# Two norms in a row computed from one pair of sums, and gate weights that stand still in TensorE, on one core

## The reference, cut to what matters

```python
# end of the first block
h = h + g2 * swiglu(hn, ffn_w1[1], ffn_w3[1], ffn_w2[1])
x = rms_norm(h, final_g)                 # x: the residual that the second block adds to
# start of the second block
xn = rmsnorm(x, norm_mix_2)              # rmsnorm(x, g) = x * rsqrt(mean(x*x) + 1e-6) * g
# xn @ w_in_2 gives, among others:
#   keys and values for compression      (feature tiles 12 to 15 of what is called f1 here)
#   the queries and the other keys       (feature tiles 0 to 11 of f1)
#   64 gate columns: beta, decay, head gates (called tm0 here)
```

## Time and profile before

| | |
|---|---|
| median of 3 runs | 1251.72 us (1245.33 to 1254.25) |
| the profiled execution | 1253.79 us, span 1252.0 us |
| PE busy | 1175.9 us, 94% |
| DVE busy | 815.5 us, 65% |
| ACT busy | 590.6 us, 47% |
| POOL busy | 77.7 us, 6% |
| DMA | 226.41 MB, mean 181 GB/s |
| mean granted TensorE clock | 0.964 of full |

### The profile page before, as it was taken

How to read it: one execution, slowest core, us unless ns; L and a number is a source line. 1 busy time by engine, 2 the same in 40 slices (tenths; PEclk the granted TensorE clock), 3 DMA queues, 4 the chain that set the end, 5 groups by cost and what they waited for, 6 DMA issues and landing times.

```text
span 1252.0 us, 24371 instructions
## 1 busy us (share of the span) xinstructions
PE 1175.9 (94%) x10460; PEld 1119.1 (89%) x10460; DVE 815.5 (65%) x1487; ACT 590.6 (47%) x1085; POOL 77.7 (6%) x94
## 2 busy tenths in 40 slices
PE   5888799999996999999997999998999999999999
PEld 2687689999995999999997888887998999899999
DVE  3874759988885566554454578887764575777543
ACT  2434546445445444444444466763333355556442
POOL 0000010000011000000100001111520001000000
PEclk9889999999998999999698899998999999999999
DMA  9660638898891647642244242221212555755520
GB/s 389 266 256 2 258 146 346 342 357 319 333 349 43 232 170 274 202 172 69 72 182 171 75 142 70 102 102 68 70 37 85 185 183 188 272 199 202 185 107 13
DMA packets 32363, 226.41 MB, mean 181 GB/s; under 512 B 3584, under 2 KB 4736, under 8 KB 5120
## 3 DMA queue, kind: packets, MB, share of 16 engines
q1 hardware_dynamic: 30528, 221.20, 47.6%
q10 hardware_dynamic: 1728, 3.67, 0.8%
HBM read 223.80 MB, written 1.05 MB: 180 GB/s over the span
## 4 chain that ended last, share of the span: by engine, by line
PE 82%; DVE 9%; ACT 5%; DMA 2%; issue 1%; POOL 0%; SPq 0%; DVEq 0%; ACTq 0%; POOLq 0%
PE bank L546 21%; PE bank L548 20%; PE bank L547 20%; DVE sb_wlo L1772 3%; ACT sb_whi L1302 2%; PE bank L989 2%; PE bank L651 1%; PE bank L584 1%; DVE sb_ring L1806 1%; DMA sb_ring<-in_f 1%; PE bank L574 1%; DMA sb_ring<-in_ada 1%; PE bank L564 1%; PE bank L1011 1%; PE bank L980 1%
## 5 line engine op out<-in xcount | busy, mean ns | idle before, releaser
L546 PE MATMUL bank<-sb_xh,sb_whi 128*128 128x256 f32 x1496 | 427.7, 286 | 8.1 <-DVE sb_wlo L1772 5.6
L547 PE MATMUL bank<-sb_xl,sb_whi 128*128 128x256 f32 x1496 | 420.8, 281 | 0.0
L548 PE MATMUL bank<-sb_xh,sb_wlo 128*128 128x256 f32 x1496 | 420.6, 281 | 0.0
L1772 DVE TENSOR_TENSOR sb_wlo<-sb_ring,sb_whi 128x1024 fp32r<-128x1024 f32 (+1 forms) x201 | 244.2, 1221 | 140.5 <-ACT sb_whi L1302 139.8
L546 PEld LDWEIGHTS bank<-sb_xh,sb_whi 128*128 128x128 f32 x1496 | 286.3, 191 | 16.7 <-issue 12.6
L547 PEld LDWEIGHTS bank<-sb_xl,sb_whi 128*128 128x128 f32 x1496 | 288.0, 192 | 0.1
L548 PEld LDWEIGHTS bank<-sb_xh,sb_wlo 128*128 128x128 f32 x1496 | 286.1, 191 | 0.0
L1302 ACT ACTIVATE sb_whi<-sb_ring 128x1024 fp32r<-128x1024 f32 (+1 forms) x201 | 210.7, 1052 | 95.0 <-PE bank L548 84.1
L1772 DVE TENSOR_TENSOR sb_wlo<-sb_more,sb_whi 128x1024 fp32r<-128x1024 f32 x108 | 131.0, 1223 | 72.9 <-ACT sb_whi L1302 72.9
L548 PE MATMUL bank<-sb_hh,sb_wlo 128*128 128x256 f32 x608 | 168.7, 277 | 0.0
L546 PE MATMUL bank<-sb_hh,sb_whi 128*128 128x256 f32 x608 | 168.7, 277 | 0.0
(11 more groups left out here) (349 smaller groups left out, 1863.8 us busy)
## 6 DMA issues: line engine op xcount, KB each, us to landing
sb_more<-in_w SPq DMA_DIRECT2D x34, 1024.0 KB, 6.8
sb_ring<-in_w SPq DMA_DIRECT2D x32, 1024.0 KB, 5.9
sb_ring<-in_adaT SPq DMA_DIRECT2D x26, 1024.0 KB, 7.7
sb_ring<-in_f SPq DMA_DIRECT2D x24, 1024.0 KB, 4.9
sb_more<-in_adaT SPq DMA_DIRECT2D x18, 1024.0 KB, 9.1
sb_ring<-in_gn SPq DMA_DIRECT2D x8, 1024.0 KB, 4.9
sb_ring<-in_gd SPq DMA_DIRECT2D x8, 1024.0 KB, 4.9
sb_ring<-in_up SPq DMA_DIRECT2D x8, 1024.0 KB, 5.8
```

What stands on the lines that cost most here:

```text
L546: te.matmul(out, wh, rh, start=start, stop=False, skip_group_check=skip)
L547: te.matmul(out, wh, rl, start=False, stop=False, skip_group_check=skip)
L548: return te.matmul(out, wl, rh, start=False, stop=stop, skip_group_check=skip)
L1772: ve.tensor_tensor(lo, x, hi.bitcast(F32), ALU.subtract).then_inc(*lo_dve.up(n))
```

## The change

Both norms are found from `h` itself. With r the mean square of `h` plus 1e-6, the first norm gives h·final_g/√r, and its mean square is mean((h·final_g)²)/r. So ACT writes a second set of squares, of h·final_g, into `z8` during the last down projection; POOL adds that set too; PE sums both; and the second norm's scale is a product of two small numbers. `apply` for the second block now works on `h` with the gain `final_g`·`norm_mix_2` and the product of both deviations. The residual (the first norm's result, written over `h`) moves behind `apply`, two tiles at a time between DVE's splits for f1 tiles 12 to 15, with its own spread on PE.

f1 tiles 12 and 13 are computed by `opening`. The gates move behind tile 15: 24 matmuls in which the gate weights stand (128x64) and 256 tokens move, then, behind tile 0, two transposes. The work on the gates after that is in three pieces, and `blocks(0)` comes behind the second one on DVE. The plan of chunks has tm0 behind the first two f1 chunks. `spread` runs no `idle` beside the residual's spread; the sums have two `idle` in all as before.

```diff
-    add("tm0", 1, 512)
-    for i, n in ((0, 4), (4, 2), (6, 2)):
+    for i, n in ((0, 2), (2, 2), (4, 2), (6, 2)):
         add("f1", n, first=i)
-        if i < 6:
-            add("cw1", 2, split=False, first=i // 2)
+        if i == 0:
+            add("tm0", 1, 512)
+        elif i < 6:
+            add("cw1", 2, split=False, first=i - 2)
...
+            def mean_squares_last():
+                banks = [take(RA, ("ms", norm, 0), (dve, "finvar")) for norm in ("fin", "mix2")]
...
+                P.wait_ge(*pool.at("sum", "fin", KT - 2))
+                part(0, 0, sq, True, False)
+                P.wait_ge(*pool.at("sum", "mix2", KT - 2))
+                part(1, 0, z8, True, False)
+                idle(1)
+                P.wait_ge(*act.at("sq", "fin", KT - 1))
+                part(0, KT - 1, sq, False, True).then_inc(*pe.up(("ms", "fin")))
+                P.wait_ge(*act.at("sq", "mix2", KT - 1))
+                part(1, KT - 1, z8, False, True).then_inc(*pe.up(("ms", "mix2")))
+                idle(1)
...
-            for k in range(KT):
-                mean_square("mix2", k)
-            spread("mix2")
-            u, _ = F.take("tm0")
...
-            for t in range(2):
-                ps = take(RG, ("gt", t), (dve, ("gt", t)))
...
-                    end = mm3(ps[:, 0:64], xh[:, k, q], xl[:, k, q], hi[:, c], lo[:, c], k == 0, k == KT - 1)
+            spread("mix2", 0)
+            def gates():
...
+                    end = mm3(ps, hi[:, c], lo[:, c], xh[:, k, :], xl[:, k, :], k == 0, k == KT - 1)
+            def gates_turned():
+                ps = take(RA, "gt", (dve, "gt"))
+                P.wait_ge(*act.at("gtT"))
+                for t in range(2):
+                    end = te.transpose(ps[:, t * 64:(t + 1) * 64], ta_of("gtT")[0:64, t * 128:(t + 1) * 128], ident[0:64, 0:64])
...
-            for j in (12, 13, 14, 15, 0, 1, 2, 3):
+            kv = [take(RG, ("f1", j), (act, ("f1", j)))[:, 0:T] for j in (12, 13)]
+            opening("f1", "mix2", [(ps, True) for ps in kv], [("f1", j) for j in (12, 13)])
+            spread("fin")
+            for j in (14, 15):
+                f1(j)
+            gates()
+            f1(0)
+            gates_turned()
+            for j in (1, 2, 3):
                 f1(j)
             hidden(0)
# ACT, last down projection
+                    if layer == 1:
+                        A.wait_ge(*pe.at("poolm"))
+                        sc.activation(z8[:, j, :], h[:, j, :], ACT.Square, scale=C("fg")[:, j:j + 1]).then_inc(*act.up(("sq", "mix2", j)))
# ACT, behind it
+            A.wait_ge(*dve.at("fina"))
+            sc.activation(d[:, 0, :], d[:, 0, :], ACT.Sqrt).then_inc(*act.up())
+            A.wait_ge(*dve.at("finvar"))
+            sc.activation(d[:, 1, :], d[:, 1, :], ACT.Sqrt, bias=C("eps"), scale=1.0 / D).then_inc(*act.up("finsd"))
...
-            for j in (12, 13, 14, 15, 0, 1, 2, 3):
+            for j in (12, 13, 14, 15):
+                f1(j)
+            gates()
+            f1(0)
+            gates2()
+            f1(1)
+            gates3()
+            for j in (2, 3):
                 f1(j)
# DVE
+            V.wait_ge(*pe.at("ms", "fin"))
+            ve.tensor_scalar(da, ps_of(("ms", "fin", 0))[:, 0:2], 1.0 / D, EPS, ALU.mult, ALU.add).then_inc(*dve.up())
+            ve.reciprocal(ra, da).then_inc(*dve.up("fina"))
+            V.wait_ge(*pe.at("ms", "mix2"))
+            ve.tensor_tensor(db, ps_of(("ms", "mix2", 0))[:, 0:2], ra, ALU.mult).then_inc(*dve.up("finvar"))
+            V.wait_ge(*act.at("finsd"))
+            ve.reciprocal(flat(dev[:, 5:7, :]), flat(dev[:, 5:7, :])).then_inc(*dve.up(("rs", "fin")))
+            ve.tensor_tensor(dev[:, 0, :], da, db, ALU.mult).then_inc(*dve.up(("rs", "mix2")))
+            apply("mix2", h, scl[:, 5, :], None, xh, xl)
...
             for j in (12, 13, 14, 15):
                 f1(j)
+                residual_normed(2 * (j - 12))
+                residual_normed(2 * (j - 12) + 1)
+            weights("tm0")
+            f1(0)
+            gates()
+            f1(1)
+            gates2()
             blocks(0)
-            for j in (0, 1, 2, 3):
-                f1(j)
+            f1(2)
+            gates3()
+            f1(3)
# POOL
+            for k in range(1, KT - 1):
+                for norm, src in (("fin", sq), ("mix2", z8)):
+                    G.wait_ge(*act.at("sq", norm, k))
...
+                    gp.tensor_tensor(src[:, 0, :], src[:, 0, :], src[:, k, :], ALU.add).then_inc(*pool.up(("sum", norm, k)))
```

More of the change, by code:

```diff
@@ L597, in mean_square_rest, with part, spread @@
                 end.then_inc(*pe.up(("ms", norm)))
-            def spread(norm):
+            def mean_squares_last():
+                banks = [take(RA, ("ms", norm, 0), (dve, "finvar")) for norm in ("fin", "mix2")]
+                def part(i, k, src, first, last):
+                    for t in range(2):
+                        end = te.matmul(banks[i][:, t:t + 1], src[:, k, t * 128:(t + 1) * 128], ones[:, 0:1],
+                                        start=first and t == 0, stop=last, skip_group_check=True)
+                    return end
+                P.wait_ge(*pool.at("sum", "fin", KT - 2))
[8 more added lines that the diff above has]
+                idle(1)
+            def spread(norm, slot=None):
                 ps = take(RO, ("spread", norm), (dve, ("used", norm)))
-                idle(2 * (norm not in ("mix0", "ctx")))
+                idle(2 * (norm not in ("mix0", "ctx", "fin")))
                 P.wait_ge(*dve.at("rs", norm))
                 for t in range(2):
-                    end = te.matmul(ps[:, t * 128:(t + 1) * 128], columns(dev[:, NORMS.index(norm), t:t + 1]), ident, start=True, stop=True)
+                    end = te.matmul(ps[:, t * 128:(t + 1) * 128], columns(dev[:, NORMS.index(norm) if slot is None else slot, t:t + 1]), ident, start=True, stop=True)
                 end.then_inc(*pe.up(("spread", norm)))
-                idle(2 * (norm not in ("mix0", "ctx")))
+                idle(2 * (norm not in ("mix0", "ctx", "fin")))
             def pace():
@@ L2027, in f1_inverse, with gates3 @@
+            def gates3():
+                V.wait_ge(*act.at("dtln"))
+                V.wait_ge(*dve.at("dtmax"))
+                ve.tensor_tensor(gg[:, :, :], gg[:, :, :], gw[:, 1, :, :], ALU.add).then_inc(*dve.up())
+                V.wait_ge(*act.at("ea"))
+                V.wait_ge(*dve.now())
+                for t in range(2):
+                    ve.scalar_tensor_tensor(gg[:, t, :], gg[:, t, :], -1.0, ea[:, :], ALU.mult, ALU.mult).then_inc(*dve.up(("gg", t)))
             def f1_inverse(j):
```

117 lines of the change are left out of this document (61 added, 56 removed).

## The result

The changed kernel takes **1240.57 us** (median of 6 runs, 1237.43 to 1243.29), the kernel before 1250.58 in 6 runs beside it: ratio 0.9929, 95% interval 0.99 to 0.9958. Two more groups of runs of the same changed kernel gave 1238.19 (4 runs, ratio 0.9892, interval 0.9853 to 0.9932) and 1237.87 (6 runs, 0.9882, 0.9835 to 0.993). Over all 16 the median is 1238.8, with single runs from 1227.2 to 1244.5; the kernel before has 1249.8 in its 55. The forecast of 1237.3 is 1.5 us off in time. It rested on 1251.7 for the kernel before, though, so the gain is 11.0 us where 14.4 was forecast: that the time came so close is partly luck.

The account below looks back on a forecast made before the run. PE, at work 94% of the span, was taken as the bound. Norm 7.2 plus opening, gates and clock 9.4, less 2.2 for a longer wait, gave 14.4 us less: 1237.3 us on the median, range 1231 to 1246.

Parts of the forecast that it names:

- Part 1: Seam between the blocks: one pass of sums, root and spread for both norms starts `apply` 7.2 us earlier, at 599.6.
- Part 2: Behind `apply`: opening has tiles 12 and 13 done at 606.6; residual's spread adds 0.45, its multiplies cost nothing under tiles.
- Part 3: Gates behind tile 15: 24 matmuls take 2.8 us in place of 10.7; tile 0 ends at 618.35.
- third rival: Clock stays at half through the new opening, costing 8.3 us: gain 6.1, 1245.6 us; chance 0.11.
- The sum by parts: Gain up to `f1_spread(1)`: norm 7.2, opening, gates and clock 9.4, longer wait takes 2.2 back: 14.4 us.
- Part 4: From tile 0's end, a 13.35 us chain over ACT and DVE delays `f1_spread(1)` to 631.7; PE waits 3.7, not 1.5.
- first rival: The wait at `f1_spread(1)` lets the clock fall, costing 3.0 us: gain 11.4, 1240.3 us; chance 0.30.
- everything behind `hidden(0)` as now, earlier by 14: Sign of being right: the program after `hidden(0)` keeps its pattern and moves as a whole, 14 us earlier.

Follow-up runs that it names:

- again: The changed kernel run and traced once more without an edit; 1238.19 us (4 runs).
- again_5: The changed kernel run and traced another time without an edit; 1237.87 us (6 runs).
- before_inverse: The kernel before, with DVE's inverse root ahead of the split for odd f1 tiles and nothing of the change; 1243.54 us (12 runs).
- inverse_first: The changed kernel with DVE's inverse root ahead of the next chunk's split for odd f1 tiles; 1226.75 us (4 runs).
- inverse_blocks: The edit of `inverse_first` on the changed kernel, and also `blocks(0)` ahead of tile 1's small operations on DVE; 1223.73 us (4 runs).
- blocks_idles: `inverse_blocks` with four idle rows on PE ahead of the second `f1_spread`; 1223.27 us (6 runs).
- gates_old: The changed kernel with the gates as 48 matmuls of 64 columns at the new place, without ACT copy and transposes; 1245.81 us (10 runs).

## Why the prediction was right, and where it wasn't

**Part 1, the norm.** Forecast: both sets of sums, bank, three idles, spread at 599.1, `apply` at 599.6. With the 1.45 us by which this execution is late these are 600.55 and 601.05; the trace has 600.38 and 601.03. The 7.2 us are met to 0.1, the idles held by their bank included (`[0.32 <-DVE sb_dev L2058]`). Undone, they cost 7.5 at the end of the chain. In `again` and `again_5` the clock falls to 0.50 for 3.4 us under the sums and `apply` starts 0.9 and 1.7 later: what the first trace doesn't show and the sum didn't count.

**Part 2, the opening and the residual.** Its last product and the residual's spread were due at 606.6, with the shift 608.05; the spread starts at 608.08. The residual costs nothing, and the cover named for it is the reason (2.05 us without it).

**Part 3, the gates and the clock.** 2.8 forecast, 2.72 measured, the clock at 1.00 for the whole stretch: the third rival did not come. The end of tile 0 was due at 619.80 and the transposes behind it start at 619.53. The sum by parts has a slip of 0.1 here (16.7 less 7.2 is 9.5, not 9.4), on which nothing hangs.

**Part 4, the wait.** Its chain has the right members in the right order and is 0.9 too long: 13.35 forecast, 619.53 to 631.94 = 12.41 measured. Tanh and exp took 0.75 (621.61 to 622.36) where 1.40 was read from the earlier trace rows (619.50 to 620.90), a stretch in which ACT also sat idle for DVE. So PE waits 2.70 us instead of 3.7. The table load was followed by the next instruction 1.30 us after its start, without a gap ahead. The drain of the Trainium skill ("ScalarE: Activation LUTs", What ACT_TABLE_LOAD costs) shows in no row here, and the rows decide.

At `f1_spread(1)` the gain is then 15.65 us (51.00 - 35.35) in the first trace and 14.7 on average over the three. **14.4** was forecast. Undone one at a time, norm, gates and opening cost 7.5, 4.5 (counted from `apply`) and 2.8 us at this point, 14.8 together; such prices need not add up, but these leave little for another cause.

**What failed** is one choice and one assumption. The choice: the clock in the wait was costed at 0 (first rival, 0.30). It fell, for 3.4 us, in all three traces. By the end of `hidden(0)` 1.4 of the 15.65 us are gone (55.32 - 41.07 = 14.25), half of the rival's price of 3.0, since `f1_spread` and the first part of `hidden(0)` alone fell into it. The Trainium skill ("TensorE: Matmul & The Clock Gate", Why this matters for your kernels) warns of gaps between bursts of matmuls. The traces agree: the drop stands behind an empty wait of 2.7 to 2.9 us in six of seven, and behind the same place filled with idles in none of two.

The assumption: "everything behind `hidden(0)` as now, earlier by 14". From `hidden(0)` to the end the kernel before took 598.7 us and the three traces of the changed one 601.0, 603.3 and 600.5. This is 1.8 to 4.6 us given back where no instruction differs. About half of it lies in the stretches of 0.50: 24 us of them in before and 27, 31 and 24 in the three, of which half is lost. They come behind the same stretches of the program in each trace, to within some 10 us, but their number (four or five) and their lengths differ. Theory B of `again` wanted the same places and the same lengths in each; the lengths are not the same. The rest is open.

Is it the change that does this? There is one trace of before, but others bear on it. The traces with the change, whole or in part, and no edit to the inverse root (nine, the three included) have 598.1 to 603.3 here, so before's 598.7 is at the short end of what the changed order shows too. And with the inverse root first the kernel before has 593.5, the changed one 592.7, 591.5 and 590.9 (`before_inverse` against `inverse_first`, `inverse_blocks` and `blocks_idles`; the last two have a further edit). That speaks for a lucky trace of before rather than for a harm that the change always does; it doesn't settle it.

Taken together, on average over the three traces the gain is 14.7 us at `f1_spread(1)`, 13.2 at the end of `hidden(0)` and 10.4 at PE's last matmul, and the medians of the runs say 11.0.

**Against the median** the forecast took 1251.7 from three runs; 55 runs have 1249.8. These 1.9 us too much and the 3.4 us too much of gain nearly cancel, which is luck. The range (1231 to 1246) holds all three medians.

## What to carry to other kernels

When PE waits for a tiny result, read what stands right ahead of that result on its engine: here a split of 1.2 us, itself waiting for a DMA, held an inverse root of 0.2 us, and moving one line gave 8 us before the change and some 11 after it. Count the gain of a seam from the last instruction ahead of it in both traces, not from the start of the program, and cost a new empty wait of PE of near 3 us as the wait and a stretch of half clock behind it. The half clock can also come without a wait: in `blocks_idles` and `gates_old` narrow matmuls stood shortly ahead of it. A tile that takes its input piece by piece as it comes already overlaps it, so fusing two tiles into an opening saves one tile and no more.
